# Two transformer blocks on one core: the first two input units formed from the raw input and scaled per token afterwards

## What is computed

```python
def rms_norm(x, g):
    xf = x.astype(jnp.float32)
    y = xf * lax.rsqrt(jnp.mean(xf * xf, axis=-1, keepdims=True) + EPS)
    return (y * g.astype(jnp.float32)).astype(x.dtype)

        h = rms_norm(x, norm1_g[layer])
        proj = h @ w_in[layer]
        q, k, v, glu_a, glu_b = jnp.split(proj, splits, axis=-1)
        ...
        c = glu_a * jax.nn.sigmoid(glu_b)
        c = causal_depthwise_conv(c, conv_dw_w[layer], conv_dw_b[layer])
```

## Time and profile before

| what | before |
|---|---|
| median of 3 runs | 1237.76 us (1237.38 to 1238.04) |
| profiled execution, its own time | 1236.94 us |
| its span | 1235.2 us |
| TensorE busy | 1199.7 us, 97% of the span |
| VectorE, ScalarE, GpSimd busy | 589.3, 481.4, 503.7 us |
| granted clock, mean | 0.994 |

### The profile page before, as it was taken

How to read it: one execution, slowest core, us unless ns; L and a number is a source line. 1 busy time by engine, 2 the same in 40 slices (tenths; PEclk the granted TensorE clock), 3 DMA queues, 4 the chain that set the end, 5 groups by cost and what they waited for, 6 DMA issues and landing times.

```text
span 1235.2 us, 15272 instructions
## 1 busy us (share of the span) xinstructions
PE 1199.7 (97%) x5668; PEld 977.6 (79%) x5668; DVE 589.3 (48%) x850; ACT 481.4 (39%) x699; POOL 503.7 (41%) x285
## 2 busy tenths in 40 slices
PE   7998989999999999999999999999999999999997
PEld 6876757888888888888877788887888888888885
DVE  5698974264444544000555678953544445440003
ACT  6245474333333333122455734434433333332113
POOL 3541030744434444444673332217444443444442
PEclk9999999999999999999999999999999999999999
DMA  5421120322333322223232211213223333223211
GB/s 176 137 86 52 35 68 1 103 71 99 102 102 102 102 90 96 88 101 102 69 111 68 69 35 34 70 35 103 89 82 102 102 102 100 87 102 102 102 68 69
DMA packets 84598, 105.39 MB, mean 85 GB/s; under 512 B 2019, under 2 KB 77130, under 8 KB 84554
## 3 DMA queue, kind: packets, MB, share of 16 engines
q1 hardware_dynamic: 84394, 104.53, 25.3%
q10 hardware_dynamic: 160, 0.26, 0.1%
HBM read 102.43 MB, written 2.10 MB: 85 GB/s over the span
## 4 chain that ended last, share of the span: by engine, by line
PE 87%; DVE 5%; ACT 3%; POOL 2%; issue 2%; DMA 1%; SPq 0%; POOLq 0%; ACTq 0%; DVEq 0%
PE ps L1518 18%; PE ps L1519 18%; PE ps L1520 18%; PE ps L1841 9%; PE ps L1846 9%; PE ps L2022 3%; PE ps L1606 3%; PE ps L1975 2%; DVE cy L1073 2%; PE ps L1652 2%; POOL w_lo L444 1%; DMA w_raw<-in_w_in 1%; ACT w_hi L561 1%; PE ps L1897 1%; PE ps L1673 1%
## 5 line engine op out<-in xcount | busy, mean ns | idle before, releaser
L444 POOL TENSOR_TENSOR w_lo<-w_raw,w_hi 128x1024 fp32r<-128x1024 f32 x178 | 428.0, 2408 | 584.0 <-ACT w_hi L561 514.7
L1518 PE MATMUL ps<-h_hi,w_hi 128*128 128x512 f32 x936 | 370.8, 396 | 3.9 <-POOL w_lo L444 1.6
L1519 PE MATMUL ps<-h_lo,w_hi 128*128 128x512 f32 x936 | 364.8, 390 | 0.0
L1520 PE MATMUL ps<-h_hi,w_lo 128*128 128x512 f32 x936 | 364.8, 390 | 0.0
L561 ACT ACTIVATE w_hi<-w_raw 128x1024 fp32r<-128x1024 f32 x190 | 200.0, 1055 | 327.1 <-PE ps L1520 145.4
L1518 PEld LDWEIGHTS ps<-h_hi,w_hi 128*128 128x128 f32 x936 | 175.9, 188 | 47.4 <-issue 6.8
L1520 PEld LDWEIGHTS ps<-h_hi,w_lo 128*128 128x128 f32 x936 | 175.7, 188 | 37.3
L1519 PEld LDWEIGHTS ps<-h_lo,w_hi 128*128 128x128 f32 x936 | 176.0, 188 | 35.1 <-issue 0.5
L1208 DVE TENSOR_TENSOR ps<-ps,rbs 128x512 f32<-128x512 f32 x88 | 61.5, 699 | 172.0 <-PE ps L1520 171.6
L743 ACT ACTIVATE cv<-ps,par 128x512 f32<-128x512 f32 x44 | 34.3, 779 | 183.9 <-DVE ps L1208 161.9
L1174 DVE TENSOR_TENSOR xT<-xT,ps 128x512 f32<-128x512 f32 x24 | 16.4, 685 | 154.9 <-PE ps L1846 106.7
(11 more groups left out here) (292 smaller groups left out, 1662.7 us busy)
## 6 DMA issues: line engine op xcount, KB each, us to landing
w_raw<-in_w_up SPq DMA_DIRECT2D x33, 1024.0 KB, 5.1
w_raw<-in_w_down SPq DMA_DIRECT2D x22, 1024.0 KB, 4.7
w_raw<-in_w_in SPq DMA_DIRECT2D x21, 1024.0 KB, 5.2
w_raw<-in_w_gate SPq DMA_DIRECT2D x11, 1024.0 KB, 5.2
w_raw<-in_w_out SPq DMA_DIRECT2D x8, 1024.0 KB, 4.9
xtok<-in_x SPq DMA_DIRECT2D x4, 512.0 KB, 5.1
out_dram<-obuf SPq DMA_DIRECT2D x8, 256.0 KB, 2.0
sq<-in_final_norm_w SPq DMA_DIRECT2D x1, 512.0 KB, 5.9
```

The source lines that it names most:

```text
L444: pool.tensor_tensor(unit_view(w_lo, at, down), unit_raw(at, down), unit_view(w_hi, at, down).bitcast(F32), ALU.subtract).then_inc(s_lo, 1)
L1518: pe.matmul(ps[:, bank, :], whi, hi, start=first, stop=False, skip_group_check=True)
L1519: pe.matmul(ps[:, bank, :], whi, lo, start=False, stop=False, skip_group_check=True)
L1520: mm = pe.matmul(ps[:, bank, :], wlo, hi, start=False, stop=last, skip_group_check=True)
```

## The change

The norm weights are applied to the raw transposed input: r = xT * gain, split into r_hi (ScalarE) and r_lo (VectorE), in the space of xs and xtok. Units 0 and 1 are formed from r, in a new order (`first_pair`), and VectorE multiplies the two PSUM banks by the tokens' factors afterwards (`rescale`), before ScalarE evicts them. The factors are spread over the partitions by one matmul (bank 5), which ScalarE copies to rbs. `token_scale` and the 32 scaled transposes are dropped. For all later units h_hi and h_lo are still wanted: VectorE forms htmp = xT * gain * rbs and h_lo, ScalarE h_hi, eight times each, after r_lo. ScalarE's casts of units 2 and 3 stand before its h_hi. TensorE multiplies units 2 and 3 together, tile by tile, as h_lo comes, and transposes the parameters after them. SyncE issues weight pair 1 directly behind pair 0. The squares of x go to qk instead of xs.

```diff
@@ SyncE
             pair(0, cols(w_in, in_cols[0]), first=True)
+            pair(1, cols(w_in, in_cols[1]), first=True)
...
-            pair(1, cols(w_in, in_cols[1]), first=True)
@@ ScalarE
-            lead(0)
             for half in range(2):
                 act.wait_ge(s_xr, 2 * TT - 1 + half)
                 act.activation(xT[:, 4 * half:4 * half + 4, (TT - 1) * P:], chunks(ps[:, 2 + half, :]),
                                ACT.Copy).then_inc(s_xTa, 1)
             act.wait_ge(s_par, 1)
+            act.wait_ge(s_xT, 6)
+            act.wait_ge(s_xTa, 2)
             for k in range(KD):
                 if k == 1:
+                    lead(0)
+                if k == 2:
                     lead(1)
-                act.wait_ge(s_xp, k + 1)
-                act.activation(h_hi[:, k, :], ps[:, 4 + k % 4, :], ACT.Copy,
-                               scale=par[:, 0, C_N1 + k:C_N1 + k + 1]).then_inc(s_hhi, 1)
+                act.activation(r_hi[:, k, :], xT[:, k, :], ACT.Copy,
+                               scale=par[:, 0, C_N1 + k:C_N1 + k + 1]).then_inc(s_rhi, 1)
+            act.wait_ge(s_rb0, 1)
+            act.activation(rbs[:], ps[:, 5, :], ACT.Copy).then_inc(s_rbs0, 1)
             lead(2)
             lead(3)
+            for k in range(KD):
+                act.wait_ge(s_ht0, k + 1)
+                act.activation(h_hi[:, k, :], htmp[:, k % 2, :], ACT.Copy).then_inc(s_hhi, 1)
...
-                    act.wait_ge(s_used, u + 1)
+                    if u < 2:
+                        act.wait_ge(s_rw, u + 1)
+                    else:
+                        act.wait_ge(s_used, u + 1)
@@ VectorE
+            dve.wait_ge(s_r0, TT)
+            dve.tensor_tensor(diag[:], ident[:, None, :].to_broadcast([P, TT, P]),
+                              rstd[:, :, None].to_broadcast([P, TT, P]), ALU.mult).then_inc(s_dg0, 1)
...
+            dve.wait_ge(s_xTa, 2)
             for k in range(KD):
-                if k < 2:
-                    rest(k)
+                if k in (1, 2):
+                    rest(k - 1)
+                dve.wait_ge(s_rhi, k + 1)
+                dve.scalar_tensor_tensor(r_lo[:, k, :], xT[:, k, :], par[:, 0, C_N1 + k:C_N1 + k + 1],
+                                         r_hi[:, k, :].bitcast(F32), ALU.mult, ALU.subtract).then_inc(s_rlo, 1)
+
+            def normalized_lo(k):
                 dve.wait_ge(s_hhi, k + 1)
-                dve.scalar_tensor_tensor(h_lo[:, k, :], ps[:, 4 + k % 4, :], par[:, 0, C_N1 + k:C_N1 + k + 1],
-                                         h_hi[:, k, :].bitcast(F32), ALU.mult, ALU.subtract).then_inc(s_hlo, 1)
+                dve.tensor_tensor(h_lo[:, k, :], htmp[:, k % 2, :], h_hi[:, k, :].bitcast(F32),
+                                  ALU.subtract).then_inc(s_hlo, 1)
+
+            def rescale(u):
+                dve.wait_ge(s_used, u + 1)
+                dve.wait_ge(s_rbs0, 1)
+                dve.tensor_tensor(ps[:, u, :], ps[:, u, :], rbs[:], ALU.mult).then_inc(s_rw, 1)
+
+            dve.wait_ge(s_rbs0, 1)
+            for k in range(KD):
+                if k >= 2:
+                    dve.wait_ge(s_hlo, k - 1)
+                dve.scalar_tensor_tensor(htmp[:, k % 2, :], xT[:, k, :], par[:, 0, C_N1 + k:C_N1 + k + 1],
+                                         rbs[:], ALU.mult, ALU.mult).then_inc(s_ht0, 1)
+                if k >= 1:
+                    normalized_lo(k - 1)
+            normalized_lo(KD - 1)
+            for u in range(2):
+                rescale(u)
@@ TensorE
-            for m in range(4):
-                scaled_transposes(m)
...
+            def first_pair():
+
+                for k in range(2):
+                    pe.wait_ge(s_rhi, k + 1)
+                    for c in range(2):
+                        pe.wait_ge(s_hi, c + 1)
+                        raw_product(k, c, w_hi, r_hi, first=(k == 0))
+                    pe.wait_ge(s_rlo, k + 1)
+                    for c in range(2):
+                        raw_product(k, c, w_hi, r_lo)
+                pe.wait_ge(s_dg0, 1)
+                pe.matmul(ps[:, 5, :], ones[:], diag[:].rearrange("p t n -> p (t n)"),
+                          start=True, stop=True, skip_group_check=True).then_inc(s_rb0, 1)
+                for c in range(2):
+                    pe.wait_ge(s_lo, c + 1)
+                    for k in range(2):
+                        raw_product(k, c, w_lo, r_hi)
+                for k in range(2, KD):
+                    pe.wait_ge(s_rlo, k + 1)
+                    for c in range(2):
+                        raw_product(k, c, w_hi, r_hi)
+                        raw_product(k, c, w_hi, r_lo)
+                        raw_product(k, c, w_lo, r_hi, last=(k == KD - 1))
+
+            pe.wait_ge(s_xT, 6)
+            pe.wait_ge(s_xTa, 2)
+            first_pair()
+            pe.wait_ge(s_lo, 4)
             for k in range(KD):
                 pe.wait_ge(s_hlo, k + 1)
                 for c in range(2):
-                    if k == 0 and c == 1:
-                        pe.wait_ge(s_lo, 2)
-                    unit_mms(c, U_IN + c, k, k == 0, k == KD - 1, used=(k == KD - 1))
-                if k < 4:
-                    scaled_transposes(k + 4)
-            pe.wait_ge(s_xTa, 2)
+                    unit_mms(2 + c, U_IN + 2 + c, k, k == 0, k == KD - 1, used=(k == KD - 1))
             pe.wait_ge(s_prow, 16 * NPROW)
...
-            unit(U_IN + 2, 2)
-            pe.wait_ge(s_par, 5)
-            unit(U_IN + 3, 3)
```

More of the change, by code:

```diff
@@ L120, in hybrid_blocks_kernel @@
                 xtok = sb("xtok", [P, TT, DM], stack=start)
-                xs = sb("xs", [P, TT, DM], stack=start)
+                r_hi = sb("r_hi", [P, KD, SEQ], F32R, stack=start)
                 prow = sb("prow", [P, 4, P], stack=start)
+            with ExitStack() as reuse:
+                r_lo = sb("r_lo", [P, KD, SEQ], F32R, stack=reuse)
             zl = sb("zl", [P, 4, ZW], stack=early)
@@ L178, in hybrid_blocks_kernel @@
         s_r0 = sem("s_r0")
-        s_xs = sem("s_xs")
+        s_dg0 = sem("s_dg0")
+        s_rb0 = sem("s_rb0")
+        s_rbs0 = sem("s_rbs0")
+        s_rhi = sem("s_rhi")
+        s_rlo = sem("s_rlo")
+        s_ht0 = sem("s_ht0")
+        s_rw = sem("s_rw")
         s_pp = sem("s_pp")
         s_par = sem("s_par")
-        s_xp = sem("s_xp")
         s_xT = sem("s_xT")
@@ L565, in _ @@
                 act.wait_ge(s_xin[t], 16)
-                act.activation(xs[:, t, :], xtok[:, t, :], ACT.Square, accum_out=ss0[:, t:t + 1]).then_inc(s_ss0, 1)
-            lead(0)
+                act.activation(qk[:, 2 * t:2 * t + 2, :].rearrange("p a n -> p (a n)"), xtok[:, t, :],
+                               ACT.Square, accum_out=ss0[:, t:t + 1]).then_inc(s_ss0, 1)
             for half in range(2):
@@ L974, in token_variance @@
                 dve.tensor_scalar(stat[:, t:t + 1], ss0[:, t:t + 1], 1.0 / DM, EPS, ALU.mult, ALU.add).then_inc(s_v0, 1)
-            def token_scale(t):
-                dve.wait_ge(s_r0, t + 1)
-                dve.tensor_scalar(xs[:, t, :], xtok[:, t, :], rstd[:, t:t + 1], None, ALU.mult).then_inc(s_xs, 1)
             raw(0)
@@ L987, in _ @@
             dve.tensor_copy(par[:, 0, 0:KD], ps[:, 7, 0:KD]).then_inc(s_par, 1)
-            token_scale(0)
             token_variance(2)
             raw(4)
-            token_scale(1)
+            raw(5)
             token_variance(3)
-            raw(5)
-            token_scale(2)
-            token_scale(3)
+            dve.wait_ge(s_r0, TT)
+            dve.tensor_tensor(diag[:], ident[:, None, :].to_broadcast([P, TT, P]),
+                              rstd[:, :, None].to_broadcast([P, TT, P]), ALU.mult).then_inc(s_dg0, 1)
             def rest(at):
@@ L1015, in _ @@
                 dve.wait_ge(s_pp, len(PROWS))
-                dve.tensor_copy(par[:, t, c:n], ps[:, 3, t * P + c:t * P + n]).then_inc(s_par, 1)
+                dve.tensor_copy(par[:, t, c:n], ps[:, 4, t * P + c:t * P + n]).then_inc(s_par, 1)
             dve.wait_ge(s_par, 5)
@@ L1019, in _ @@
             dve.wait_ge(s_pp, len(PROWS) + 1)
-            dve.tensor_copy(selT[:], ps[:, 5, 0:P]).then_inc(s_cdve, 1)
+            dve.tensor_copy(selT[:], ps[:, 6, 0:P]).then_inc(s_cdve, 1)
             def spread(n):
@@ L1575, in spread, with raw_product @@
                           start=True, stop=True, skip_group_check=True).then_inc(s_rb, 1)
-            pe.wait_ge(s_lo, 1)
+            def raw_product(k, c, w, a, first=False, last=False):
+                mm = pe.matmul(ps[:, c, :], unit_view(w, U_IN + c, False)[:, k, :], a[:, k, :], start=first, stop=last,
+                               skip_group_check=True)
+                if last:
+                    mm.then_inc(s_used, 1)
+            def first_pair():
[24 more added lines that the diff above has]
+            pe.wait_ge(s_lo, 4)
             for k in range(KD):
@@ L1580, in _ @@
                 for c in range(2):
-                    if k == 0 and c == 1:
```

(13 more changed lines are left out.)

## The result

The changed kernel takes 1242.33 us (median of 11 runs, 1240.02 to 1244.46) against 1236.95 us for the kernel before on the same occasions (11 runs, 1235.19 to 1239.10). The ratio is 1.0042, with a 95% interval of 1.003 to 1.0054: slower by 0.42%. The forecast was 1242.5 us. The profiled execution took 1242.95 us against 1236.94, spans 1241.2 and 1235.2, so its 6.0 us are to be found.

A forecast was written before the change was run, and what follows sets the result against it. TensorE was taken to bound the kernel up to 97.76 us, with 0.34 us slack before unit 12. Late taps 3.9 plus clock 0.8 gave +4.7 on 1237.76, so 1242.5 us, range 1237.2 to 1245.4.

The forecast's parts named there:

- Start and first pair: Units 0 and 1: products start at 15.5 us and end near 27.1 us, a saving against about 29.5 before.
- The norm: Second pair's htmp and h_lo on VectorE: two waits of 2.35 us for GpSimd's subtractions, 4.6 us lost.
- The first take and the gates: First rescale ends at 37.3 us; gates wait for GpSimd's subtractions, end at 47.2 us, taps start 4.25 us late.
- Rival B: Collision in the norm alone; gates meet GpSimd idle or once, 1238.3 to 1239.9 us; chance 0.17.
- Unit 12: Taps of the first two tiles end at 88.25 us, TensorE waits 3.4 us, then is 3.9 us behind.
- Beyond: After unit 12: VectorE's 2.77 us idle before 97.76 swallows its own lateness, up to 1.6 us; the 3.9 stay.
- The clock: Half clock after TensorE's new waits of 2.3 and 3.4 us: 0.8 us taken, bounds 0 and 3.3.
- Rival A: No port collision: unit 4 starts at 38.45 us, 2.4 us ahead, kernel faster at 1235.4 us; chance 0.12.

The follow-up runs named there:

- The run with the idle transposes: Changed kernel plus 32 transposes of the identity, results unread, on TensorE before the first product: 1240.84 us, ratio 1.0038.
- the gates first: Changed kernel, but GpSimd after subtracting for unit 4 waits until both gate multiplies of the first two tiles are done: 1238.3 us, ratio 1.0004.
- all but the gates: Changed kernel with 32 unread transposes before the first product and VectorE subtracting for units 2 and 3, GpSimd not held back: 1239.45 us, ratio 1.0016.
- the copies in the kernel before: Kernel before with six unneeded copies of an idle PSUM bank on VectorE ahead of its first gate: 1243.81 us, ratio 1.0046.
- all three edits: Changed kernel with 32 unread transposes, VectorE subtracting for units 2 and 3, GpSimd waiting after unit 4 for the gates: 1236.23 us, repeated 1236.09 us.
- the first experiment: Changed kernel with GpSimd held after unit 4's subtraction until the first two tiles' gate multiplies are done: 1238.3 us, ratio 1.0004.

## Why the prediction was right

The forecast was 1242.5, the measured median 1242.33. That the two are 0.2 us apart is luck: of the difference to before, 5.4 us were measured and 4.7 forecast, and the median of before was 0.8 us lower with 11 runs than with the 3 that the forecast started from. The path that the forecast named, from the gates over the taps to unit 12, is the one that the runs show. Step by step:

- **Start and first pair: wrong.** The step put 47 products at 0.228 us each. TensorE had idled 2.6 and 1.0 us for the two casts and ran at 0.50 from 15 to 21.6 us, so a product of the first burst cost 0.43 us, the spreading matmul 1.71 instead of 0.87, and the first pair ended at 30.45 instead of 27.1 us. The term that was wrong is the clock, which the sum looked at only behind the two later waits. It was masked: TensorE then never waited for h_lo, nor the 2.3 us forecast before unit 4, and unit 4 began at 41.74 (41.3 forecast). The run with the idle transposes puts the forecast's picture back, wait for GpSimd included, and is not measurably faster.
- **The norm: mechanism right, size of the waits too large.** Two operations were stretched, by 1.13 and 2.02 us, not two by 2.35. But rbs was ready at 21.5 instead of 19.7 us behind the slow matmul, and with it the casts of units 2 and 3, so VectorE idled 0.31 us for rbs and 1.00 for h_hi 0, which the forecast didn't have. That makes 4.5 us lost against 4.6, and h_lo 7 began at 36.2 us (36.0 forecast). Two errors cancel, which is luck.
- **The first take and the gates: right.** The first rescale ended at 37.5 (37.3), the gates began at 42.9 (42.3) and ended at 47.3 (47.2). The forecast let them wait for the eviction of unit 3 only; the parameter copies were ready at the same moment, and the run with units 2 and 3 in turn shows that these can be the later of the two. Rival B's 7.2 us of GpSimd's work from 38.9 on leave out unit 4's own subtraction; the four took 10.37 us from 39.19.
- **Unit 12: right.** The taps ended at 88.4 (88.25), TensorE waited 2.9 us (3.4) and was 4.1 us behind (3.9). Three runs show the cause from three sides: the gates first, all but the gates, and the copies in the kernel before.
- **Beyond: right.** The second gates took 3.10 us and VectorE still idled 3.35 us before the scales of q and k.
- **The clock: inside the bounds, twice the value taken.** 1.7 us in the profiled execution, where 0 to 3.3 was the bound and 0.8 was taken. The odds were near even: behind the wait before unit 12 the clock fell in four profiled executions (waits of 2.9, 2.9, 2.9 and 3.9 us) and stayed at 1.00 in three (1.3, 2.2 and 3.4 us). But the price of one drop, 1.67 us, was read from one execution. The same 20 matmuls took 4.18 to 5.38 us over all the profiled executions, 1.5 to 2.7 us more than at full clock, so 3.3 us wasn't a safe upper bound for two.

Rival A priced what is possible without the collision at 2.4 us ahead at unit 4. The first run with all three edits has it there, at 38.47 us instead of 40.82, but its second 16 raw transposes had started 1.1 us earlier than those of before (8.49 against 9.59). In the second such run they started 0.5 us later (10.12) and unit 4 at 39.93, 0.9 us ahead. Counted from these transposes both are 1.2 to 1.4 us ahead, little more than half of A's price. And not all of it reaches the end: at 95.54 us the first of the two is 2.2 us ahead of the earlier trace rows's 97.76, at the end 1.0. Nearly all of this went at its next long wait, behind which the 20 matmuls took 5.38 us instead of 4.39, as they do in other executions too. Rival B was brought about in the first experiment: 1238.3 against its 1238.3, though B counted from 1237.76 for before and the median of before was 1237.17 on that occasion.

The Trainium skill's rule on the ports (SBUF — State Buffer, section "Who interferes with whom") held in both of its halves: two inputs in SBUF wait, one doesn't, as the rows with htmp from PSUM show (2.77 us against 0.75). The Trainium skill says there that the order of issue decides who blocks; here, with both queues full, the engines took turns, so that two gates waited for two subtractions.

## What to carry to other kernels

When a change moves work in time, list what two engines do at the same moment afterwards: VectorE operations with two SBUF inputs against GpSimd's long ones each waited for the one that was running, here 0.9 to 2.1 us of its 2.4. Look for the places with little slack that the chain of waits doesn't show, like the 0.34 us before unit 12; a gain of TensorE alone ahead of such a place is worth little (the idle transposes by themselves weren't measurably faster), and a delay of the other engine's work counts in full (4.32 us of copies gave a wait of 3.9). And before taking filler off TensorE's queue ahead of a burst, count the half clock that the gap may bring, although it may hide behind another wait.

## What was not expected of the hardware

- The first 16 raw transposes took 3.3 to 3.8 us in every profiled execution but the second 16 took 1.96 or 1.97 in most, 2.55 in one and 3.56 to 3.67 in others, of the same code, while the column of the granted clock read 1.00 in both. A transposition cost 0.23 or 0.12 us. In the kernel before, the load of the weights, there at 12.41 us, hides most of it: in the run with the six copies the second 16 took 3.57 us, 1.6 more than in the earlier trace rows, and the first product started at 16.36 us instead of 15.95, 0.4 later. In the changed one ScalarE's last copies of xT, and with them r_hi and the casts, wait for these transposes.
- With the second weight load of 1 MB issued directly behind the first, SyncE took 4.79 us to issue the next small load, where it had taken 0.86. Nothing waited for it here.
